# Stacking B with K and U with V on the partitions of a chunked recurrence, and moving part of the state work among the grams

## Chip, cores and metric

One core of a Trainium2 chip. The metric is the device time of one execution in microseconds, lower is better. All arithmetic of the part in question is fp32.

## What is computed

The program is three layers on 1024 latent and 256 context tokens of width 1024. The change touches only the recurrence of the first layer, an RWKV-7 scan over 1280 tokens with 8 heads of 64, run in both directions:

```python
def step(S, inp):
    r_t, w_t, k_t, v_t, a_t, b_t = inp
    sa = jnp.einsum('bhij,bhj->bhi', S, a_t)
    S = S * w_t[:, :, None, :] + sa[..., None] * b_t[:, :, None, :] + v_t[..., None] * k_t[:, :, None, :]
    return S, jnp.einsum('bhij,bhj->bhi', S, r_t)
```

## The kernel before, in words

The recurrence is `phase_scan` (line 822). It runs alone: a barrier of all engines ends the phase before and the one after begins behind another. The tokens are cut in chunks of 64; two chunks make a block of 128 tokens, and there are 10 blocks. Both directions (d = 0 forward, 1 backward) go side by side on the same engines. Inside a block, chunk q lies on partitions 64q to 64q+63. An fp32 matmul shows in the trace as two weight loads and two matmuls, on separate rows (PEld and PE).

For each block there is "new" work, which needs no state, and for the block before it "old" work, which carries the state. They are interleaved by hand: each engine has a loop over n from 0 to 10 whose body is a fixed list of calls, new ones for block n and old ones for block n-1. Engines wait for one another by semaphores (`done(engine, name, d, n, r)`); within an engine the order is the list's.

New work of block n:

- SP loads A and R (`ar`, line 880), B and K (`bk`, 884) and V (`vt`, 886), transposed, that is channels on partitions, three DMAs for each direction; a block's loads are issued one block ahead. Before the first gram come also six constants (line 896), which stand on SP's queue after the loads of block 0.
- `gram(n, 0)` multiplies B, `gram(n, 1)` K, with A and R together (line 929), in 64x64 tiles: 64 matmuls in all. VectorE's `masked` (1131) multiplies each PSUM bank by a triangular mask, giving `mB` and `mK`. K's gram waits for B's masks, since both use the banks bA and bB.
- `turn_v` and `turn_bk` transpose V (937), B and K (947) to tokens on partitions; ScalarE copies them out (`turned_v`, `turned_bk`, recorded at 1246, like all its copies). `mask_v` (958) multiplies K's masked gram by V; ScalarE copies the product to `MV`.
- The inverse of the unit triangular matrix of each chunk is built up: ScalarE copies the 32x32 diagonal blocks (`diagonal`), VectorE makes the start value (`base`), GpSimd (1120) the block products' left operand. Then four levels: `level_p` (972), VectorE's mask (1150), `level_z` (982), VectorE's sum and transpose (1158, 1160), each with a copy of half of Z by ScalarE (`swapped`). At the end `last_p` (994) and `last_z` (1006) in 32x32 tiles.

Old work, twice a block (e = 0, 1, one chunk each), each time four steps of TensorE that depend on one another: `state_w` (1024), VectorE adds MV (1184); `state_u` (1037), ScalarE copies U; `state_sums` (1055), 64 matmuls in 64x64 tiles that add U and V parts in PSUM; `state_read` (1063). VectorE then renews the state (1189, 1194) and adds the output (1200). The lists of before put W of e = 0 behind `level_p(n, 0)`, and the others one by one behind the groups that follow.

The gram of block n+1 waits for `zf` of block n, VectorE's last step (1173).

## Time and profile before

| | us |
|---|---|
| median of 3 runs (3467.09 to 3473.81) | 3473.52 |
| the profiled execution's own time | 3474.22 |
| its span | 3472.4 |
| the recurrence in it, first load issued to last output | 595.3 to 1090.7 |

The profile is of one execution. Times in it count from the span's start. PE is TensorE's matmuls, PEld its weight loads, DVE VectorE, ACT ScalarE, SP the queue that issues DMAs. In the timeline a row is one instruction or a run of like ones (x count), and a bracket says how long the engine was idle before it and what ended that; "issue" means that nothing which the profile shows held it. In the windows view a row is a stretch with the busy time of each engine and, in brackets, its instructions, the granted TensorE clock (1.00 is 2.4 GHz), the share of DMA engines busy and GB/s.

### The profile page before, as it was taken

The page shows a single profiled execution, that of the slowest core. Times are in us where ns is not written, and L with a number is a line of the kernel's source. Part 1 is how long each engine was busy: PE and PEld are TensorE (multiplying, and loading weights), DVE is VectorE, ACT ScalarE, POOL GpSimd, SP SyncE. Part 2 cuts the span into 40 slices and gives each one's busy share as a digit, 9 for nine tenths or more (in the row PEclk, how much of TensorE's full clock was granted, in tenths as well). Part 3 has the DMA queues.
Part 4 walks back from the last instruction along what each step waited for, and adds up shares of the span by engine and source line. Part 5 has one row for each costly group of instructions (what it writes and reads, how often), then busy time and mean ns, then how long its engine had stood idle before and what let it go on. Part 6 is the DMA issues. An engine that isn't in the chain of part 4 may idle for free. (4 is left out here: it accounts for less than half of the span.)

```text
span 3472.4 us, 63359 instructions
## 1 busy us (share of the span) xinstructions
PE 3105.7 (89%) x27018; PEld 2569.8 (74%) x27018; DVE 2013.4 (58%) x2899; ACT 1442.3 (42%) x2207; POOL 409.7 (12%) x293
## 2 busy tenths in 40 slices
PE   8999997777775799898999999999677899999999
PEld 5878886766664679766899987777445778888887
DVE  6746345566564532253555534666343588888787
ACT  4434433333332333256444432443354454545443
POOL 0122221000000122110000012312011100000000
PEclk9999999798897899999999999999898999999999
DMA  8432223233214221324211114112111322222853
GB/s 295 137 127 105 97 90 131 63 76 76 76 46 155 103 86 42 140 75 162 81 60 54 42 37 146 58 52 97 59 49 34 125 79 79 85 79 73 303 164 122
DMA packets 184566, 343.88 MB, mean 99 GB/s; under 512 B 11488, under 2 KB 116064, under 8 KB 180832
## 3 DMA queue, kind: packets, MB, share of 16 engines
q1 hardware_dynamic: 161248, 252.80, 21.8%
q0 software_dynamic: 23040, 87.04, 7.4%
q8 instruction: 215, 3.52, 0.4%
q14 instruction: 63, 0.52, 0.1%
HBM read 243.72 MB, written 96.08 MB: 98 GB/s over the span
## 5 line engine op out<-in xcount | busy, mean ns | idle before, releaser
L60 PE MATMUL ev_ps<-h_hi,even_ring_hi 128*128 128x512 f32 (+1 forms) x792 | 288.0, 364 | 1.3 <-DVE late_area L806 1.3
L61 PE MATMUL ev_ps<-h_lo,even_ring_hi 128*128 128x512 f32 (+1 forms) x792 | 280.4, 354 | 0.0
L62 PE MATMUL ev_ps<-h_hi,even_ring_lo 128*128 128x512 f32 (+1 forms) x792 | 280.4, 354 | 0.0
L60 PE MATMUL ff_ps<-ff_op,ff_w_hi 128*128 128x512 f32 x672 | 263.5, 392 | 13.6 <-DVE ff_w_lo L3504 10.7
L62 PE MATMUL ff_ps<-ff_op,ff_w_lo 128*128 128x512 f32 x672 | 262.8, 391 | 0.0
L61 PE MATMUL ff_ps<-ff_op,ff_w_hi 128*128 128x512 f32 x672 | 262.7, 391 | 0.0
L60 PEld LDWEIGHTS ev_ps<-h_hi,even_ring_hi 128*128 128x128 f32 x792 | 149.6, 189 | 39.9 <-issue 19.6
L3071 ACT ACTIVATE ma_e<-ma_s,ma_nm 128x1280 f32<-128x1280 f32 x64 | 84.9, 1327 | 216.3 <-DVE ma_nm L3107 216.3
L61 PEld LDWEIGHTS ev_ps<-h_lo,even_ring_hi 128*128 128x128 f32 x792 | 149.7, 189 | 21.7 <-issue 1.7
L62 PEld LDWEIGHTS ev_ps<-h_hi,even_ring_lo 128*128 128x128 f32 x792 | 149.6, 189 | 21.3
L60 PEld LDWEIGHTS ff_ps<-ff_op,ff_w_hi 128*128 128x128 f32 x672 | 127.1, 189 | 41.2 <-DVE ff_w_lo L3504 14.5
L3045 PE MATMUL ma_o<-ma_pt,ma_v 128*128 128x128 f32 x1280 | 153.2, 275 | 0.0
L3045 PEld LDWEIGHTS ma_o<-ma_pt,ma_v 128*128 128x128 f32 x1280 | 147.9, 192 | 0.0
L61 PEld LDWEIGHTS ff_ps<-ff_op,ff_w_hi 128*128 128x128 f32 x672 | 127.0, 189 | 26.6 <-issue 0.2
L62 PEld LDWEIGHTS ff_ps<-ff_op,ff_w_lo 128*128 128x128 f32 x672 | 126.9, 189 | 26.5
L103 POOL TENSOR_TENSOR even_ring_lo<-even_ring_raw,even_ring_hi 128x1024 fp32r<-128x1024 f32 x33 | 94.2, 2854 | 417.3 <-ACT even_ring_hi L98 417.3
L60 PE MATMUL ff_ps<-ff_w_hi 128*128 128x512 f32 x336 | 131.2, 390 | 2.6 <-DVE ff_w_lo L3584 1.8
L62 PE MATMUL ff_ps<-ff_w_hi,ff_w_lo 128*128 128x512 f32 x336 | 130.8, 389 | 0.0
L61 PE MATMUL ff_ps<-ff_w_lo,ff_w_hi 128*128 128x512 f32 x336 | 130.7, 389 | 0.0
L3537 DVE SCALAR_TENSOR_TENSOR h<-h,cols 128x1023 f32<-128x1023 f32 x96 | 122.6, 1278 | 0.5 <-ACT h L3401 0.4
L3103 DVE TENSOR_REDUCE ma_mx<-ma_s 128x1 f32<-128x1024 f32 x64 | 78.2, 1222 | 69.7 <-PE ma_s L3025 69.7
L103 POOL TENSOR_TENSOR second_ring_lo<-second_ring_raw,second_ring_hi 128x1024 fp32r<-128x1024 f32 x32 | 79.1, 2473 | 307.9 <-ACT second_ring_hi L98 307.9
(566 smaller groups left out, 8362.3 us busy)
## 6 DMA issues: line engine op xcount, KB each, us to landing
w_up_raw<-in_w_up SPq DMA_DIRECT2D x48, 512.0 KB, 4.6
w_up_raw<-in_w_down SPq DMA_DIRECT2D x34, 512.0 KB, 5.0
even_ring_raw<-in_ev_w_in POOLq DMA_DIRECT2D x33, 512.0 KB, 3.9
late_area<-in_ada_w SPq DMA_DIRECT2D x32, 512.0 KB, 5.2
ffn_mid<-h POOLq DMA_DIRECT2D x24, 512.0 KB, 2.9
ff_mem<-ffn_mid SPq DMA_DIRECT2D x24, 512.0 KB, 11.0
ar<-late_area SPq DMA_DIRECT2D x8, 1280.0 KB, 5.6
bk<-late_area SPq DMA_DIRECT2D x8, 1280.0 KB, 8.0
```

The lines of the kernel that those rows point to most:

```text
L60: nc.tensor.matmul(out, w_hi, x_hi, start=start, stop=False, skip_group_check=resumed)
L61: nc.tensor.matmul(out, w_hi, x_lo, start=False, stop=False, skip_group_check=resumed)
L62: return nc.tensor.matmul(out, w_lo, x_hi, start=False, stop=stop, skip_group_check=resumed)
L103: nc.gpsimd.tensor_tensor(ring.lo[:, a % 2], ring.w[:], ring.hi[:, a % 2].bitcast(F32), ALU.subtract).then_inc(ring.lo_done, 1)
L3045: mm = nc.tensor.matmul(po[:, u % 2, 0:P], v[:, h % 2, t], pt[:, u % 2, t * P:t * P + P], start=t == 0, stop=t == NT - 1)
L3071: nc.scalar.activation(e[:, s % 2], ps[:, 0:T], ACT.Exp, bias=nm[:, s % 2:s % 2 + 1], accum_out=sm[:, s % 2:s % 2 + 1]).then_inc(exps, 1)
L3103: nc.vector.tensor_reduce(mx[:, b, 0:1], ps[:, 0:2 * BANK], AX, ALU.max).then_inc(maxed, 1)
L3537: stt(out=a[:, i:LAT], in0=rows[x_][:, 0:LAT - i], scalar=col(g, "conv_ffn_w", 48 * (2 - i) + at), in1=a[:, i:LAT], op0=ALU.mult, op1=ALU. ...
```

## The change

B and K of a chunk are stacked: `bk` holds, for each pair of heads and chunk q, 64 tokens of one beside 64 of the other (K first for q = 1), so one matmul of 64x128 tiles gives both grams of a chunk. `gram(n, x)` over B and K becomes `gram(n, q)` over the chunks, 32 matmuls instead of 64. The two masked grams lie stacked in `M`, on 128 partitions, and U and V of a chunk in `UV`: U on the half of the chunk, V on the other. `state_sums` then contracts over 128 partitions, one matmul where two were added in PSUM: 32 matmuls for each e instead of 64, in 128x64 tiles. V's loads swap the chunks of a block. The loads of `bk` and `vt` are cut by chunk: seven DMAs for each direction and block instead of three, with rows of 64 tokens instead of 128. ScalarE copies V in four pieces of 64 partitions, and the diagonal blocks of chunk 0 before those of chunk 1; GpSimd's product is made for each chunk.

The lists change too. On TensorE `state_w(n-1, 0)` goes between the two grams, `state_u(n-1, 0)` between `turn_v` and `turn_bk`, `state_sums(n-1, 0)` ahead of `level_p(n, 0)` and `state_read(n-1, 0)` behind it; the second half's W and U follow levels 1 and 2, its sums `level_p(n, 3)`. VectorE and ScalarE follow.

```diff
-        ar, bk, vt = sb("ar", [P, 3, 2, 4, 2, P]), sb("bk", [P, 2, 2, 4, 2, P]), sb("vt", [P, 2, 2, 4, P])
-        mB, mK = sb("mB", [P, 2, 2, 8, 2, CH]), sb("mK", [P, 2, 2, 8, 2, CH])
-        V, Bt, MV, Zf = sb("V", [P, 2, 2, BANK]), sb("Bt", [P, 2, 2, 2, BANK]), sb("MV", [P, 2, 2, BANK]), sb("Zf", [P, 2, 2, 8, CH])
+        ar, bk, vt = sb("ar", [P, 3, 2, 4, 2, P]), sb("bk", [P, 2, 2, 4, 2, 2, CH]), sb("vt", [P, 2, 2, 4, P])
+        M, UV = sb("M", [P, 2, 2, 2, 8, 2, CH]), sb("UV", [P, 2, 2, 2, 8, CH])
+        Bt, MV, Zf = sb("Bt", [P, 2, 2, 2, BANK]), sb("MV", [P, 2, 2, BANK]), sb("Zf", [P, 2, 2, 8, CH])
         dg, Z, X, P5 = (sb(x, [P, 2, 8, 32]) for x in ("diag", "Z", "X", "P5"))
         mD, Pm = sb("mD", [P, 2, 8, CH]), sb("Pm", [P, 2, 8, CH])
         Zs = sb("Z_swapped", [P, 2, 4, 32])
-        W, U = sb("W", [P, 2, BANK]), sb("U", [P, 2, BANK])
+        W = sb("W", [P, 2, BANK])
...
-                        sp.dma_start(bk[:, n % 2, d].rearrange("c p k t -> c (p k) t"),
-                                     g.bkT[d].rearrange("c p k t -> c (p k) t")[:, :, at:at + P]).then_inc(ld[d, n % 2], 16)
-                        sp.dma_start(vt[:, n % 2, d], g.vT[:, :, at:at + P]).then_inc(ld[d, n % 2], 16)
+                        for q in range(2):
+                            to = at + CH * q
+                            for x in range(2):
+                                sp.dma_start(bk[:, n % 2, d, :, q, x ^ q], g.bkT[d][:, :, x, to:to + CH]).then_inc(ld[d, n % 2], 16)
+                            sp.dma_start(vt[:, n % 2, d, :, half(1 - q)], g.vT[:, :, to:to + CH]).then_inc(ld[d, n % 2], 16)
...
-                def gram(n, x):
+                def gram(n, q):
                     for d in range(2):
-                        if x == 0:
-                            pe.wait_ge(ld[d, n % 2], 48 * (n // 2 + 1))
+                        if q == 0:
+                            pe.wait_ge(ld[d, n % 2], 112 * (n // 2 + 1))
                             if n:
                                 done(pe, "Pev", d, n - 1)
                                 done(pe, "zf", d, n - 1)
                         else:
-                            done(pe, "mB", d, n)
+                            done(pe, "mk0", d, n)
                         settle()
                         for p in range(4):
-                            for q in range(2):
-                                for h in range(2):
-                                    r, c = half(h), half(q)
-                                    last = mm((bA, bB)[h][d][c, 128 * p:128 * p + 128], bk[r, n % 2, d, p, x, c], ar[r, n % 3, d, p, :, c],
-                                              start=True, stop=True)
-                        last.then_inc(S[("gB", "gK")[x], d], 2)
+                            for h in range(2):
+                                r, c = half(h), half(q)
+                                last = mm((bA, bB)[h][d][:, 128 * p:128 * p + 128], bk[r, n % 2, d, p, q].rearrange("c x t -> c (x t)"),
+                                          ar[r, n % 3, d, p, :, c], start=True, stop=True)
+                        last.then_inc(S[("g0", "g1")[q], d], 2)
...
-                            last = nc.tensor.transpose((bB, bA)[x][d][:, 128 * p:128 * p + 128], bk[:, n % 2, d, p, x], g.ident[:])
+                            last = nc.tensor.transpose((bB, bA)[x][d][:, 128 * p:128 * p + 128],
+                                                       bk[:, n % 2, d, p, x].rearrange("c x t -> c (x t)"), g.ident[:])
...
-                        for j, (p, h) in enumerate(HEADS):
+                        for j in range(8):
                             for q in range(2):
-                                c = half(q)
-                                last = mm(bB[d][c, 64 * j:64 * j + 64], mK[c, n % 2, d, j, 0],
-                                          V[c, n % 2, d, 128 * p + 64 * h:128 * p + 64 * h + 64], start=True, stop=True)
+                                k = half(1 - q)
+                                last = mm(bB[d][half(q), 64 * j:64 * j + 64], M[k, n % 2, d, q, j, 0], UV[k, n % 2, d, q, j],
+                                          start=True, stop=True)
...
-                        for x in (2, 3, 0, 1):
-                            for h in range(2):
-                                for d in range(2):
-                                    c, r, j = half(ORDER[d][e]), half(h), 4 * h + p
-                                    o, ov = half(j), half(2 * p + h)
-                                    at = 64 * p + (256 if x >= 2 else 0)
-                                    lhs, rhs = ((U[c, d, o], mB[c, b, d, j, 1]), (V[c, b, d, ov], mK[c, b, d, j, 1]),
-                                                (Bt[c, b, d, 0, ov], U[c, d, o]), (Bt[c, b, d, 1, ov], V[c, b, d, ov]))[x]
-                                    mm(bD[d][r, at:at + 64], lhs, rhs, start=x % 2 == 0, stop=x % 2 == 1)
+                        for h in range(2):
+                            for d in range(2):
+                                q, r, j = ORDER[d][e], half(h), 4 * h + p
+                                mm(bD[d][r, 256 + 64 * p:320 + 64 * p], Bt[:, b, d, q, half(2 * p + h)], UV[:, b, d, q, j], start=True, stop=True)
+                        for h in range(2):
+                            for d in range(2):
+                                q, r, j = ORDER[d][e], half(h), 4 * h + p
+                                mm(bD[d][r, 64 * p:64 * p + 64], UV[:, b, d, q, j], M[:, b, d, q, j, 1], start=True, stop=True)
...
                     if new:
                         gram(n, 0)
+                    if old:
+                        state_w(n - 1, 0)
+                    if new:
                         gram(n, 1)
                         turn_v(n)
+                    if old:
+                        state_u(n - 1, 0)
+                    if new:
                         turn_bk(n, 0)
                         mask_v(n)
                         turn_bk(n, 1)
-                        level_p(n, 0)
-                    if old:
-                        state_w(n - 1, 0)
-                    if new:
-                        level_z(n, 0)
-                    if old:
-                        state_u(n - 1, 0)
-                    if new:
-                        level_p(n, 1)
                     if old:
                         state_sums(n - 1, 0)
                     if new:
+                        level_p(n, 0)
+                    if old:
+                        state_read(n - 1, 0)
+                    if new:
+                        level_z(n, 0)
+                        level_p(n, 1)
                         level_z(n, 1)
                     if old:
-                        state_read(n - 1, 0)
+                        state_w(n - 1, 1)
                     if new:
                         level_p(n, 2)
                         level_z(n, 2)
                     if old:
-                        state_w(n - 1, 1)
+                        state_u(n - 1, 1)
                     if new:
                         level_p(n, 3)
                     if old:
-                        state_u(n - 1, 1)
+                        state_sums(n - 1, 1)
                     if new:
                         level_z(n, 3)
-                    if old:
-                        state_sums(n - 1, 1)
-                    if new:
                         last_p(n)
...
-                        done(pool, "mB", d, n)
                         if n:
                             done(pool, "P", d, n - 1, NL - 1)
-                        nc.gpsimd.tensor_tensor(mD[:, d], mB[:, n % 2, d, :, 0], hm[:].unsqueeze(1).broadcast_to([P, 8, CH]),
-                                                ALU.mult).then_inc(S["blocks", d], 1)
+                        for q in range(2):
+                            c = half(q)
+                            done(pool, ("mk0", "mk1")[q], d, n)
+                            nc.gpsimd.tensor_tensor(mD[c, d], M[c, n % 2, d, q, :, 0], hm[c].unsqueeze(1).broadcast_to([CH, 8, CH]),
+                                                    ALU.mult).then_inc(S["blocks", d], 1)
...
                         masked(n, 0, 0)
                         masked(n, 0, 1)
+                    if old:
+                        state_w(n - 1, 0)
+                    if new:
                         masked(n, 1, 0)
                         masked(n, 1, 1)
                         base(n)
                         level_mask(n, 0)
                     if old:
-                        state_w(n - 1, 0)
+                        state_s(n - 1, 0)
                     if new:
                         level_add(n, 0)
+                    if old:
+                        output(n - 1, 0)
+                    if new:
                         level_mask(n, 1)
                         level_add(n, 1)
                     if old:
-                        state_s(n - 1, 0)
+                        state_w(n - 1, 1)
                     if new:
                         level_mask(n, 2)
-                    if old:
-                        output(n - 1, 0)
-                    if new:
                         level_add(n, 2)
-                    if old:
-                        state_w(n - 1, 1)
-                    if new:
                         level_mask(n, 3)
                         level_add(n, 3)
                         inverse_diagonal(n)
...
-                    for d in range(2):
-                        done(act, "mB", d, n)
-                        if n:
-                            done(act, "z0", d, n - 1)
-                        for c in range(4):
-                            k, a = slice(32 * c, 32 * c + 32), 32 * (c % 2)
-                            cp(dg[k, d], mB[k, n % 2, d, :, 0, a:a + 32]).then_inc(S["diag", d], 1)
+                    for q in range(2):
+                        for d in range(2):
+                            done(act, ("mk0", "mk1")[q], d, n)
+                            if n and q == 0:
+                                done(act, "z0", d, n - 1)
+                            for c in (2 * q, 2 * q + 1):
+                                k, a = slice(32 * c, 32 * c + 32), 32 * (c % 2)
+                                cp(dg[k, d], M[k, n % 2, d, q, :, 0, a:a + 32]).then_inc(S["diag", d], 1)
 
                 def turned_v(n):
                     for d in range(2):
                         done(act, "trV", d, n)
-                        cp(V[:, n % 2, d], bA[d][:]).then_inc(S["Vev", d], 1)
+                        for q in range(2):
+                            k = half(1 - q)
+                            cp(UV[k, n % 2, d, q].rearrange("s (h p) c -> s h p c", h=2),
+                               bA[d][k].rearrange("s (p h c) -> s h p c", p=4, h=2)).then_inc(S["Vev", d], 1)
...
-                        cp(U[c, d], bC[d][c]).then_inc(S["Uev", d], 1)
+                        cp(UV[c, n % 2, d, ORDER[d][e]].rearrange("s j c -> s (j c)"), bC[d][c]).then_inc(S["Uev", d], 1)
...
                         diagonal(n)
                         turned_v(n)
+                    if old:
+                        state_u(n - 1, 0)
+                    if new:
                         turned_bk(n, 0)
                         masked_v(n)
                         turned_bk(n, 1)
                         swapped(n, 0)
                     if old:
-                        state_u(n - 1, 0)
+                        output(n - 1, 0)
                     if new:
                         swapped(n, 1)
                         swapped(n, 2)
                     if old:
-                        output(n - 1, 0)
+                        state_u(n - 1, 1)
                     if new:
                         swapped(n, 3)
-                    if old:
-                        state_u(n - 1, 1)
-                    if new:
                         corner(n)
```

## Rows read from the trace of the kernel before

**Rows 1.** The page's first part, busy us, share of the span, instructions, by engine

```profile
PE 3105.7 (89%) x27018; PEld 2569.8 (74%) x27018; DVE 2013.4 (58%) x2899; ACT 1442.3 (42%) x2207; POOL 409.7 (12%) x293
```

**Rows 2.** Windows: stretch, us, busy of PE, PEld, DVE, ACT, POOL, clock, DMA, GB/s

```profile
645.60:1063.70 418.10, 315.45 (x11736) 288.48 (x11736) 251.43 (x559) 153.54 (x378) 22.56 (x18) 0.88 0.23 58
...
786.26:798.68 12.42, 9.73 (x216) 8.12 (x217) 7.98 (x17) 7.25 (x16) 2.51 (x2) 1.00 0.97 244
...
798.69:831.98 33.29, 24.57 (x1088) 23.12 (x1089) 19.87 (x46) 9.77 (x27) 0.00 (x0) 0.84 0.04 9
...
1063.70:1090.70 27.00, 15.86 (x448) 14.82 (x448) 7.21 (x20) 3.68 (x8) 0.00 (x0) 0.62 0.08 22
```

**Rows 3.** Timeline of weight loads: start, us, what; in brackets idle before

```profile
757.11 0.13 PEld L982 LDWEIGHTS sc_bAB<-sc_Z_swapped,sc_Pm 64*64 64x64 f32 x1 [1.75 <-issue]
...
760.81 0.14 PEld L1055 LDWEIGHTS sc_bD<-sc_U,sc_Bt 64*64 64x64 f32 x2 [0.67 <-issue]
...
708.02 0.30 PEld L972 LDWEIGHTS sc_bAB<-sc_X,sc_mD 64*64 64x64 f32 x10 [2.18 <-issue]
```

**Rows 4.** Windows of weight loads, from one stall's end to the next stall's

```profile
757.11:760.80 3.69, 2.52 (x125) 1.00 0.02 4
...
760.81:764.16 3.35, 1.96 (x128) 1.00 0.02 5
...
779.97:783.82 3.85, 2.66 (x127) 1.00 0.02 4
```

**Rows 5.** Windows: line 1055 alone, and one level of block 0 with all engines

```profile
760.80:762.90 2.10, 2.08 (x124) 1.94 (x124) 1.00 0.03 8
...
622.50:625.90 3.40, 2.42 (x128) 2.26 (x128) 2.24 (x5) 2.19 (x7) 0.00 (x0) 1.00 0.76 211
```

**Rows 6.** Timeline of TensorE in the front, and at the end of that block

```profile
786.26 1.98 PE L929 MATMUL sc_bAB<-sc_ar,sc_bk 64*64 64x128 f32 x64 [0.96 <-DVE sc_Zf L1173]
...
794.81 1.35 PE L958 MATMUL sc_bAB<-sc_V,sc_mK 64*64 64x64 f32 x38 [0.44 <-issue]
...
829.85 1.74 PE L1006 MATMUL sc_bAB<-sc_Z,sc_P 32*32 32x32 f32 x64
```

**Rows 7.** Timeline of VectorE in the front: both groups of masks

```profile
788.30 1.89 DVE L1131 TENSOR_TENSOR sc_mB<-sc_bAB,sc_m 128x512 f32<-128x512 f32 x3 [0.18 <-PE sc_bAB L929]
...
791.77 1.89 DVE L1131 TENSOR_TENSOR sc_mK<-sc_bAB,sc_m 128x512 f32<-128x512 f32 x3 [0.18 <-PE sc_bAB L929]
```

**Rows 8.** Timeline of ScalarE in the front, then U's copies (lines by form)

```profile
789.62 3.49 ACT L1246 ACTIVATE sc_diag<-sc_mB 32x256 f32<-32x256 f32 x8 [4.78 <-DVE sc_mB L1131]
...
793.13 1.08 ACT L1246 ACTIVATE sc_V<-sc_bAB 128x512 f32<-128x512 f32 x2
...
L1246 ACT ACTIVATE sc_U<-sc_bC 64x512 f32<-64x512 f32 x28 | 16.6, 591 | 53.7 <-PE sc_bC L1037 53.3
```

**Rows 9.** The state's W: TensorE in a window of line 1024, one VectorE add

```profile
753.90:754.80 0.90, 0.69 (x32) 0.59 (x32) 1.00 0.13 29
...
801.74 0.42 DVE L1184 TENSOR_TENSOR sc_W<-sc_bC,sc_MV 64x256 f32<-64x256 f32 x1 [1.03 <-PE sc_bD L1024]
```

**Rows 10.** DMA issues of bk and vt; the window of one block's loads

```profile
sc_bk<-bk SPq DMA_DIRECT2D x20, 512.0 KB, 6.3
...
sc_vt<-v_even SPq DMA_DIRECT2D x20, 256.0 KB, 7.3
...
742.90:752.90 10.00, 7.65 (x156) 6.27 (x152) 6.49 (x13) 7.16 (x16) 2.51 (x2) 1.00 1.11 275
```

**Rows 11.** The start: SP's issue of the last constant, TensorE's first gram

```profile
604.95 0.43 SPq L896 DMA_DIRECT2D sc_eye<-in_eye  x1
...
608.90 2.41 PE L929 MATMUL sc_bAB<-sc_ar,sc_bk 64*64 64x128 f32 x40 [18.44 <-DMA sc_eye<-in_eye]
```

**Rows 12.** Windows at the lower clock: after the stall, and two levels of block 0

```profile
708.77:712.10 3.33, 3.19 (x107) 3.08 (x98) 3.09 (x9) 0.00 (x0) 0.00 (x0) 0.50 0.02 5
...
632.70:641.40 8.70, 8.19 (x256) 7.75 (x256) 6.07 (x13) 1.93 (x7) 0.00 (x0) 0.50 0.02 4
```

More of the change, by code:

```diff
@@ L827, in phase_scan @@
     NBC = CTX // P
-    names = ["gB", "gK", "trV", "trBK", "MV", "P", "Z", "lastP", "lastZ", "W", "U", "YS",
-             "mB", "mK", "z0", "Zbase", "X", "Pm", "Zadd", "zdiag", "zf", "Wev", "stmp", "snew", "y",
+    names = ["g0", "g1", "trV", "trBK", "MV", "P", "Z", "lastP", "lastZ", "W", "U", "YS",
+             "mk0", "mk1", "z0", "Zbase", "X", "Pm", "Zadd", "zdiag", "zf", "Wev", "stmp", "snew", "y",
              "diag", "blocks", "Uev", "Vev", "BKev", "MVev", "Pev", "y1", "Zs"]
-    reps = {"Zs": 2 * NL, "gB": 2, "gK": 2, "mB": 2, "mK": 2, "trBK": 2, "BKev": 2, "P": NL, "Z": NL, "Pm": NL, "Zadd": NL, "X": NL + 1, "diag": 4,
+    reps = {"Zs": 2 * NL, "g0": 2, "g1": 2, "mk0": 2, "mk1": 2, "Vev": 2, "blocks": 2, "trBK": 2, "BKev": 2, "P": NL, "Z": NL, "Pm": NL, "Zadd": NL, "X": NL + 1, "diag": 4,
             "W": 2, "U": 2, "YS": 2, "Wev": 4, "Uev": 2, "stmp": 2, "snew": 2, "y1": 2, "y": 2}
@@ L942, in turn_bk @@
                         if x == 0:
-                            done(pe, "mK", d, n, 1)
+                            done(pe, "mk1", d, n, 1)
                         else:
```

12 lines of the change are left out of this document (6 added, 6 removed).

## Prediction, before the changed kernel was run

> **What bounds it now.** The page's engine table [rows 1] puts TensorE at 89% of the span, but that mean says nothing about the recurrence, the only phase touched. The windows view cuts it out [rows 2]. Between 645.60 and 1063.70 us nine blocks, each carrying new work and the state work of the block before, take 418.1 us, 46.5 us a block, and TensorE is at work for 315 of them; VectorE for 251, ScalarE for 154. No engine is full, so I look for what TensorE waits for, stage by stage. A block has two stages. In the front (12.4 us, grams to the second pair of transposes) it issues 217 weight loads. In the rest (33.3 us, first `level_p` to `last_z`, the dense part) it issues 1088.
>
> The weight-load timeline of the dense part shows idle stretches of 0.7 to 2.2 us ended by "issue", by nobody's semaphore [rows 3]. They fall in the middle of a run of like instructions. The windows laid from one stall's end to the next [rows 4] count 125 to 128 weight loads each time, with as many matmuls, and last 3.35 to 3.85 us at the full clock. The work does not need that long: the 128 loads and matmuls of a level keep TensorE at work for 2.42 us [rows 5]. So a fixed number of instructions, about 256, comes at best every 3.4 to 3.9 us. I read this as TensorE waiting for its program. It fits the whole dense part: 1088/128 = 8.5 portions in 33.3 us, 3.9 each. The Trainium skill ("Runtime: NRT & Kernel Launch", Instruction fetch mechanics) says fetch comes in blocks of 256 instructions but is mostly hidden, with room for 2048 in TensorE's buffer. The size agrees with the trace, the hiding does not; by the rule the idle time would have another cause, and that is a rival below.
>
> In the front TensorE waits for VectorE's masks, then for ScalarE's copies [rows 6 to 8].
>
> **The change, part by part.** Per block, counted in weight loads (two for each fp32 matmul):
>
> *Grams stacked.* 128 loads become 64. Now 64 of 64x64 tiles with 128 columns take 1.98 us with four tiles working at once [rows 6]. The new form covers two of the four tiles with one instruction, so half as many at twice the share: I take 1.98 us again. The bounds are 0.99 us (an instruction costs what it cost) and 2.4 us. Gain 0: array time is not saved, only instructions.
>
> *State sums stacked.* 128 loads become 64, twice a block. Now 124 take 2.08 us at the full clock [rows 5], 17 ns each. In 128x64 tiles two work at once instead of four, so I take 30 ns each, 1.9 us, again no gain; bounds 1.0 and 2.6 us. Three changes of tile form a block are added in the dense part; the one from 64x64 to 32x32 at 829.85 loses the overlap that neighbours have [rows 6], about 0.1 us. Together 0.3 us.
>
> *Front, worked through from the first gram (0 = 786.26).* The first four masks end at 790.19, +3.9 [rows 7]. Direction-wise W of the old block now comes here: 0.7 us of TensorE [rows 9] in its 1.5 us wait, costing nothing; on VectorE four adds, 0.42 each, 1.5 us [rows 9], so to 5.4. The other gram is done by then. Four masks more, 0.69 + 3 x 0.60 = 2.5, end at 7.9 instead of 7.4: +0.5. ScalarE is worse off. Its eight `diag` copies used to start on the first masks and take 3.49 us [rows 8], ending at 6.9; now four of them need the second masks, start at 7.3 and end at 9.0. V becomes four copies on 64 partitions instead of two on 128. A 64x512 copy takes 591 ns [rows 8], as long as one on 128, so 2.4 us instead of 1.08: 11.4. Ahead of B's copy now stand U's two, 1.2 us [rows 8]: 12.6, B's first to 13.2. `mask_v` waits for V and B: 13.3 instead of 8.55 (794.81). So the front is longer by 4.8 us, nearly all on ScalarE. TensorE fills part of it with U0 (32 loads like W0, 0.7 us) and idles some 3.7 us after the first transposes. From `mask_v` to `level_p` it was 3.9 us (794.81 to 798.69), 0.5 us of that for ScalarE; with the first sums between, 1.9 us, it becomes some 5.2. `level_p` then starts at 18.5 at the latest instead of 12.4; since the sums also cover the wait for B's last copies, 18.0. Front: +5.6 us.
>
> *Dense part.* W0 (32), U0 (32) and sums0 (128) have left it and sums1 loses 64: 1088 - 256 = 832 loads, 6.5 portions. At 3.9 us each that is 25.4 us; plus 0.3 for the tile forms and 0.5 for the read and W between levels, 26.2 instead of 33.3: -7.1 us. The lower bound is the chain of dependences: one level without state work takes 3.4 us [rows 5], four of them 13.6, and last products, reads, W1, U1 and sums1 some 9: 22.5 us, also 6.5 x 3.45. The upper bound leaves the stalls and takes off only what W0, U0 and sums0 held, 0.7 + 0.7 + 2.1 and the 1.5 us of W on VectorE, in part side by side: 4.5 us, 28.8.
>
> *Masks' consumers.* GpSimd's two block products become four on half the partitions, 2.5 to 5.0 us [rows 10], from 7.3 to some 12 in the block, wanted at 18: nothing; cover gone, they would cost 2.5. `W1`, `U1` and the outputs move a level, none late.
>
> *DMAs.* Per block and direction, three loads become seven. They are issued a block ahead and took 10 us of a 46 us block [rows 10]; at rows of 256 B the 1.5 MB of bk and vt (of 2.5) could at worst take twice as long, 16 us: still hidden. The start has no cover. The constants stand behind load(0) on SP's queue, and the first gram waited 18.4 us for the last of them [rows 11]. Eight more issues at the shortest seen, 0.43 us [rows 11], are 3.4 us; partly these lie beside the transfers. Bounds: 0, and 60% of the 9 us of transfer, +5.4. I take +3. The Trainium skill ("DMA: Bandwidth & Descriptors", Specifications) asks for 512 B or more for line rate; by it the start would cost the +5.4.
>
> *First and last pass.* Block 0 has no state work: front +3.3 (second `diag` half and V), levels not held up by portions. +3. The last pass (27 us for 448 loads at a clock of 0.62 [rows 2]) is a chain; its sums are as long: 0.
>
> **Sum.** Nine blocks at +5.6 - 7.1 = -1.5: -13.5. Start +3, block 0 +3: -7.5; I round to -8 and set it against the profiled execution, 3474.2 us (span 3472.4), 0.7 above the median of 3473.5. That gives 3466.
>
> **Rivals.**
> *Clock falls in the new gap.* TensorE's granted clock is 1.0 or 0.5 of 2.4 GHz by stretch. It fell right after the 2.2 us stall that ended at 708.02 [rows 3, 12], and was 0.50 through block 0's levels, where no state work lies between them [rows 12]. The change makes both: an idle stretch of 3.7 us, and levels 0 and 1 with less between them. At 0.5 the level's pair of groups takes 4.35 us instead of 3.4 [rows 12, 5], hardly more than the 3.9 a portion takes anyway, so a fall there costs little; a fall at 13 us of the block, before `mask_v`, transposes and sums0, costs some 2 to 3 us of their 5. Nine times 2.3: +21, 3487. It decides from an idle stretch of about 2 us on. Against it: the front that I read kept a clock of 1.00 with a gap of 1.5 us in it [rows 2].
> *The stalls are not the program's.* By the skill's rule fewer instructions gain nothing: dense part 28.8, so +1.1 a block, +10, start and block 0 +6: 3490. Against it stands the count of 125 to 128 in all five intervals that I laid out (three stand in rows 4).
> *A smaller effect of both signs.* A third of the clock's cost, 8 us: 3474, no difference (chance: all but 0.02 of it within 0.2%).
> *Faster.* If portions come every 3.45 us once the half-clock stretches are fewer, or a stacked sum costs what an unstacked instruction did, 2.5 to 3.5 us a block more: 3440.
> *The change doesn't halve the time of what it halves* is already in the sum.
>
> **Chances.** Forecast 0.38, clock 0.25, not the program's 0.07, between 0.15, faster 0.15. A measurement of this kernel tells 0.2%, 7 us, from nothing. The forecast lies at that edge and gives 0.27 to faster and 0.11 to same; with the others: faster 0.43, same 0.24, slower 0.33. The range, from 3440 to 3492, takes in the faster case and the slower ones; 3455 to 3475 is the forecast's own.
>
> **What would show it.** Intervals of 128 loads at 3.4 to 3.9 us still, but fewer: 8.7 portions a block. L1055's successor with 64 loads in about 1.9 us. `mask_v` 13 us after the first gram, ScalarE without a pause from the second `diag` to B's copy. Block period 45.0 us. First gram 3 us later after the first load's issue. Wrong if the period grows, with a granted clock under 0.85, or if `mask_v` starts by 10 us.

## The result, and the profile after

| | before | after |
|---|---|---|
| median us (4 runs each) | 3473.47 (3467.09 to 3473.81) | 3501.67 (3500.55 to 3502.52) |
| the profiled execution's own time / span | 3474.22 / 3472.4 | 3501.81 / 3499.7 |

The changed kernel is slower: ratio 1.0083, 95% interval 1.0069 to 1.0097. The forecast was 3466, and 3501.67 lies above its range too.

The page of the changed kernel, its engines and its queue of instructions (packets, MB, share), answers to [rows 1]:

```profile
PE 3136.1 (90%) x25098; PEld 2606.0 (74%) x25098; DVE 2036.3 (58%) x2899; ACT 1455.3 (42%) x2227; POOL 436.2 (12%) x313
...
q8 instruction: 201, 3.29, 0.4%
```

TensorE has 1920 matmul records fewer and yet is busy 30 us longer. The first sign that the program fetch was read rightly stands in the second row: the page of before has 215 packets and 3.52 MB there, 14 packets of 16 KB more.

Windows of the changed kernel, columns as in [rows 2]: its blocks 1 to 9, then block 4's front and dense part, then the last pass.

```profile
650.81:1092.78 441.97, 347.42 (x10009) 323.07 (x10009) 271.99 (x559) 165.53 (x396) 46.80 (x36) 0.79 0.24 54
801.46:823.49 22.03, 16.73 (x280) 15.34 (x280) 11.90 (x21) 11.46 (x24) 5.20 (x4) 0.78 0.65 144
823.50:850.11 26.61, 21.19 (x835) 20.11 (x833) 18.45 (x42) 6.96 (x20) 0.00 (x0) 0.81 0.02 5
1092.78:1118.30 25.52, 17.06 (x320) 15.94 (x320) 5.12 (x14) 3.02 (x6) 0.00 (x0) 0.57 0.08 22
```

Nine blocks take 442.0 us where they took 418.1 [rows 2], on 1727 fewer matmul records, and the granted clock is 0.79 where it was 0.88. The dense part is shorter as expected (26.6 instead of 33.3 us). The front is 22.0 us instead of 12.4, and its clock of 0.78 is far from the 1.00 of [rows 2].

TensorE's timeline shows where in the front:

```profile
801.46 3.31 PE L930 MATMUL sc_bAB<-sc_ar,sc_bk 64*128 64x128 f32 x32 [0.23 <-DVE sc_Zf L1176]
...
806.25 2.06 PE L930 MATMUL sc_bAB<-sc_ar,sc_bk 64*128 64x128 f32 x32 [0.85 <-DVE sc_M L1134]
...
816.10 3.68 PE L960 MATMUL sc_bAB<-sc_UV,sc_M 64*64 64x64 f32 x64 [3.82 <-ACT sc_Bt L1249]
...
819.71 1.79 PE L948 MATMUL sc_bAB<-ident_sb,sc_bk 128*128 128x128 f32 x8
```

and the windows of three of its stretches, columns as above:

```profile
806.20:808.40 2.20, 2.06 (x32) 1.89 (x32) 2.14 (x6) 1.60 (x4) 1.27 (x1) 1.00 1.19 288
...
791.40:793.40 2.00, 2.00 (x64) 1.97 (x64) 0.71 (x2) 1.16 (x4) 0.00 (x0) 1.00 0.03 8
...
816.00:819.80 3.80, 3.70 (x65) 3.61 (x66) 0.00 (x0) 1.09 (x3) 0.00 (x0) 0.50 0.22 48
```

The gap of 3.82 us ahead of `mask_v` is the one that the prediction foresaw (3.7). What runs behind it runs at 1.2 GHz (granted 0.50): `mask_v` takes 3.68 us, the transposes 1.79. In each of blocks 1 to 9 `mask_v` ran at a mean granted clock of 0.50 to 0.57. At 2.4 GHz the same code takes 2.08 and 1.10 us in another run (experiment e4_warm, below). The second gram, at 2.4 GHz, takes 2.06 us with half of the instructions, and the 64 of stacked sums 2.10 from first start to last end (the window in the second row closes 0.1 us before that): those two estimates held.

ScalarE in that front:

```profile
806.13 1.74 ACT L1249 ACTIVATE sc_diag<-sc_M 32x256 f32<-32x256 f32 x4 [6.09 <-DVE sc_M L1134]
810.10 1.73 ACT L1249 ACTIVATE sc_diag<-sc_M 32x256 f32<-32x256 f32 x4 [2.23 <-DVE sc_M L1134]
811.85 2.44 ACT L1249 ACTIVATE sc_UV<-sc_bAB 64x512 f32<-64x512 f32 x4
814.19 1.20 ACT L1249 ACTIVATE sc_UV<-sc_bC 64x512 f32<-64x512 f32 x2
815.41 1.08 ACT L1249 ACTIVATE sc_Bt<-sc_bAB 128x512 f32<-128x512 f32 x2
```

It runs without a pause from 810.10 to 816.5, and `mask_v` waits at its end. V's four copies stand behind the second half of `diag`, though V's transposes were there from 810.2 on. From here on, "front" is from the first gram to `level_p(n, 0)` and "dense" is from there to the next block's first gram, each a mean over blocks 1 to 8 of the profiled execution.

| us | before | after | difference | forecast |
|---|---|---|---|---|
| issue of the first load to first gram | 13.6 | 15.4 | +1.8 | +3 |
| block 0 | 36.7 | 42.8 | +6.1 | +3 |
| blocks 1 to 9 | 418.1 | 442.0 | +23.9 | -13.5 |
| last pass, to TensorE's last matmul | 24.9 | 25.5 | +0.6 | 0 |

Together +32.4. The recurrence began 2.7 us earlier in this trace and the phases behind it are 2.4 us shorter, though the change leaves both parts alone: 27.3 us of span.

### The profile page after: what moved, and what is told of

It is laid out like the page before. It is cut to its first block and busy times, and to the rows that moved or that the text cites. A ratio compares the mean times of both kernels' runs of the same rounds, so it can differ in the third digit from the quotient of the medians.

```text
span 3499.7 us, 59639 instructions
## 1 busy us (share of the span) xinstructions
PE 3136.1 (90%) x25098; PEld 2606.0 (74%) x25098; DVE 2036.3 (58%) x2899; ACT 1455.3 (42%) x2227; POOL 436.2 (12%) x313
## 5 line engine op out<-in xcount | busy, mean ns | idle before, releaser
L60 PE MATMUL ff_ps<-ff_op,ff_w_hi 128*128 128x512 f32 x672 | 263.4, 392 | 13.6 <-DVE ff_w_lo L3511 10.7
L61 PEld LDWEIGHTS ff_ps<-ff_op,ff_w_hi 128*128 128x128 f32 x672 | 127.0, 189 | 26.6 <-issue 0.2
L62 PEld LDWEIGHTS ff_ps<-ff_op,ff_w_lo 128*128 128x128 f32 x672 | 126.8, 189 | 26.6
## 6 DMA issues: line engine op xcount, KB each, us to landing
ff_mem<-ffn_mid SPq DMA_DIRECT2D x24, 512.0 KB, 10.9
```

The lines of the kernel that those rows point to most:

```text
L60: nc.tensor.matmul(out, w_hi, x_hi, start=start, stop=False, skip_group_check=resumed)
L61: nc.tensor.matmul(out, w_hi, x_lo, start=False, stop=False, skip_group_check=resumed)
L62: return nc.tensor.matmul(out, w_lo, x_hi, start=False, stop=stop, skip_group_check=resumed)
```

## The experiments

Two theories of these 32 us of the recurrence. *Clock*: the gap that ScalarE makes ahead of `mask_v` drops TensorE to 1.2 GHz, and the work behind it, up to the next gram, pays. *Order*: the moved state work itself (sums and U in the front, thinner levels) costs it, whatever the clock. The runs below were measured beside the kernel before on the same chip, whose medians were 3474.78 (e1 to e4), 3470.72 (e6 to e9) and 3466.16 (e10 to e13). First all of them, with the stages of the profile. The stages come from one profiled execution of each, the medians from 4 to 10 executions that spread by 2 to 21 us, so differences of a few tenths of a us a block say nothing by themselves.

| run | median us | ratio, 95% | block | `mask_v` after gram | front | dense | clock front / dense |
|---|---|---|---|---|---|---|---|
| before | | | 46.5 | 9.7 | 13.1 | 33.4 | 0.91 / 0.87 |
| after | 3501.67 | 1.0083 (1.0069 to 1.0097) | 48.9 | 14.4 | 21.8 | 27.1 | 0.80 / 0.79 |
| e1_lists_only | 3479.48 | 1.0012 (1.0003 to 1.0021) | 47.4 | 11.8 | 17.0 | 30.5 | 0.90 / 0.74 |
| e2_stack_only | 3476.75 | 1.0008 (0.9999 to 1.0018) | 46.1 | 11.9 | 16.9 | 29.2 | 0.85 / 0.90 |
| e3_act_order | 3453.34 | 0.9936 (0.9920 to 0.9953) | 43.6 | 10.9 | 16.5 | 27.1 | 0.93 / 0.77 |
| e4_warm | 3469.69 | 0.9986 (0.9973 to 1.0000) | 45.6 | 13.8 | 19.3 | 26.3 | 0.96 / 0.79 |
| e6_sums_in_levels | 3461.55 | 0.9973 (0.9959 to 0.9987) | 44.8 | 11.1 | 16.1 | 28.7 | 0.91 / 0.79 |
| e7_by_direction | 3463.46 | 0.9978 (0.9966 to 0.9990) | 44.5 | 10.9 | 17.6 | 26.9 | 0.93 / 0.80 |
| e8_fill_gap | 3463.02 | 0.9973 (0.9962 to 0.9984) | 44.9 | 11.4 | 18.1 | 26.8 | 0.89 / 0.76 |
| e9_stack_act | 3447.63 | 0.9933 (0.9919 to 0.9948) | 42.7 | 9.5 | 13.3 | 29.4 | 0.98 / 0.89 |
| e10_before_act | 3491.97 | 1.0077 (1.0062 to 1.0092) | 47.7 | 9.8 | 15.5 | 32.2 | 0.88 / 0.86 |
| e11_diag_dve | 3445.98 | 0.9941 (0.9925 to 0.9958) | 43.5 | 9.5 | 13.6 | 30.0 | 0.98 / 0.86 |
| e12_many_small | 3456.93 | 0.9975 (0.9966 to 0.9985) | 44.9 | 9.5 | 13.3 | 31.6 | 0.98 / 0.90 |
| e13_few_wide | 3451.29 | 0.9961 (0.9948 to 0.9974) | 43.6 | 9.5 | 13.3 | 30.3 | 0.98 / 0.91 |

**The two halves of the change apart.** e1_lists_only is the kernel before with the changed lists of TensorE, VectorE and ScalarE and nothing stacked; e2_stack_only is the changed kernel with the lists of before.

```diff
 # e1, TensorE's list of before.py (e2: the same lines the other way round, in after.py)
                     if new:
                         gram(n, 0)
+                    if old:
+                        state_w(n - 1, 0)
+                    if new:
                         gram(n, 1)
                         turn_v(n)
...
```

> The kernel before with the changed kernel's three lists, nothing stacked. Theory (ScalarE's longer queue in the front plus a clock fall in the gap cost more than the saved portions of 256 instructions give): here V is still two copies and all eight diagonal copies start on the first masks, so mask_v starts about 10 us after the first gram instead of 14.6, the clock stays at 1.00 in the front, and the dense part loses 192 of 1088 weight loads (1.5 portions): block about 44 us, 3450 us in all, faster than both. Rival A (the moved state work is what hurts, because it stood in useful places before and kept the clock up between the levels): 3485 or more. Rival B (the lists do nothing): 3473.

> The changed kernel's stacking with the lists of before. Theory: ScalarE still makes four copies of V and the late diagonal copies, so mask_v starts 11.5 to 12 us after the first gram (8.55 before), with a gap of some 3 us that lets the clock fall; the dense part has 960 weight loads (7.5 portions of 3.9 us, 29 us): block 46 to 47.5 us, 3475 to 3490 us. Rival A (the lists do the harm): 3465 or less. Rival C (the stacked matmuls are slow by their form): above 3500, with the sums' 64 matmuls well over 2.1 us at the full clock.

Each half alone makes the recurrence no faster (+0.12% and +0.08%), and together they cost 0.83%. So there is something between them. e2 came out as expected. e1 was expected at 3450 and missed by 29 us: `mask_v` came at +11.8 instead of +10, and the dense part, 1.5 portions lighter, gained only 2.9 us, at a granted clock of 0.74. Its 3479 lies between rival B (3473) and rival A (3485 or more), so with the moved lists part of what the lighter dense part should give is lost. Windows of eight blocks in each, columns as before:

```profile
641.10:1020.60 379.50, 302.59 (x10435) 281.42 (x10435) 222.81 (x495) 137.76 (x336) 20.04 (x16) 0.80 0.24 62
```

```profile
649.40:1017.80 368.40, 282.22 (x8896) 259.01 (x8896) 241.55 (x495) 146.93 (x352) 41.57 (x32) 0.88 0.28 63
```

The first row is of e1, the second of e2. The lists alone bring the clock of a whole block to 0.80, the stacking alone leaves it at 0.88, as it was [rows 2]. The table says which stage: every run with the moved lists (e6 has them in part) has 0.74 to 0.80 in the dense part, every run with the lists of before 0.86 to 0.91.

**ScalarE's order.** In e3_act_order only ScalarE's list of the changed kernel is another: V and B are copied before the second half of `diag`, and U after it.

```diff
-                        diagonal(n)
-                        turned_v(n)
-                    if old:
-                        state_u(n - 1, 0)
-                    if new:
-                        turned_bk(n, 0)
+                        diagonal(n, 0)
+                        turned_v(n)
+                        turned_bk(n, 0)
+                        diagonal(n, 1)
+                    if old:
+                        state_u(n - 1, 0)
+                    if new:
                         masked_v(n)
```

> The changed kernel with ScalarE's list alone reordered: V's and B's (first) copies ahead of the second chunk's diagonal copies and of U's copies. Theory: 1.7 + 1.2 us leave the way to mask_v, which starts at 10 to 11 us instead of 14.6; the idle gap of TensorE shrinks below 1.5 us and the clock stays up in the front; block 44 to 45.5 us, 3455 to 3470 us. Rival C (slow forms) or rival A (lists): no more than the 3 us of order per block come back at best and the clock stays as it is, 3490 to 3500.

This turns the loss into a gain, 3501.67 to 3453.34 us, 2 us below what was expected. ScalarE's timeline of e3, and the windows of the same block's front and dense part:

```profile
919.45 2.44 ACT L1249 ACTIVATE sc_UV<-sc_bAB 64x512 f32<-64x512 f32 x4 [1.75 <-PE sc_bAB L938]
921.79 1.06 ACT L1249 ACTIVATE sc_Bt<-sc_bAB 128x512 f32<-128x512 f32 x2
922.88 1.72 ACT L1249 ACTIVATE sc_diag<-sc_M 32x256 f32<-32x256 f32 x4
```

```profile
912.54:927.95 15.41, 13.21 (x280) 11.84 (x280) 9.73 (x21) 9.90 (x21) 5.07 (x4) 1.00 0.91 201
927.96:955.50 27.54, 22.99 (x835) 21.67 (x832) 18.45 (x42) 8.18 (x24) 0.00 (x0) 0.74 0.03 7
```

V's copies now wait for TensorE's transposes and for nothing else. `mask_v` starts 9.9 us after this gram, and the gap ahead of it is 0.36 us instead of 3.82. The moved work stands where it stood, and its dense part has the low clock still (0.77); so the *Order* theory doesn't account for the loss.

**The same gap, filled.** e4_warm leaves ScalarE's order as in the changed kernel and only gives TensorE something to do while it waits: eight matmuls whose results nobody reads.

```diff
+                def keep_busy(n):
+                    for j in range(8):
+                        d = j % 2
+                        nc.tensor.matmul(bC[d][half(1 - ORDER[d][0]), 0:256], g.ident[half(0), 0:CH],
+                                         m1[half(0)].rearrange("s d k t -> s (d k t)"), start=True, stop=True)
...
                         turn_bk(n, 0)
+                        keep_busy(n)
                         mask_v(n)
```

> The changed kernel with eight filler matmuls (64x64 tile, 256 columns, fp32, into a free half of the state's bank) put on TensorE between turn_bk(n, 0) and mask_v, where it idles 3.8 us. They add 16 weight loads a block. Theory with the clock as the second half of the loss: mask_v, transposes and sums0 run at the full clock, mask_v's 64 matmuls in 2.1 us instead of 3.7, ScalarE's queue is as before; 2 to 3 us a block come back, 3475 to 3483 us. Rival (the clock costs nothing, since it is ScalarE that is waited for): 3500 or slower.

TensorE does more and the kernel is 32 us faster than the changed one, 3469.69, more than the 19 to 27 us that were expected. No wait was shortened by hand, since ScalarE's queue is the same, row for row, only with its times:

```profile
891.48 2.44 ACT L1256 ACTIVATE sc_UV<-sc_bAB 64x512 f32<-64x512 f32 x4
...
895.04 1.09 ACT L1256 ACTIVATE sc_Bt<-sc_bAB 128x512 f32<-128x512 f32 x2
```

```profile
882.34:900.82 18.48, 15.05 (x296) 12.88 (x295) 11.36 (x20) 11.31 (x24) 5.21 (x4) 1.00 0.72 173
900.83:926.98 26.15, 21.03 (x837) 20.12 (x834) 18.56 (x42) 6.99 (x21) 0.00 (x0) 0.80 0.02 4
```

```profile
891.84 1.94 PE L955 MATMUL sc_bC<-sc_m,ident_sb 64*64 64x256 f32 x16
895.73 2.08 PE L966 MATMUL sc_bAB<-sc_UV,sc_M 64*64 64x64 f32 x64 [1.95 <-issue]
897.75 1.10 PE L948 MATMUL sc_bAB<-ident_sb,sc_bk 128*128 128x128 f32 x8
```

These are the fillers, `mask_v` and the transposes behind it, on TensorE. The fillers split the gap: 1.95 us of it are left.

With the clock at 1.00 through the front, this block has `mask_v` at +13.39 and `level_p` at +18.49; the prediction had 13.3 and 18.0. Five of the blocks 1 to 8 look like this one, with a period of 44.6 us where 45.0 was forecast. So the clock is worth 48.9 - 45.6 = 3.3 us a block. Without most of its fall the kernel is 5 us faster than before, where 8 were forecast; the interval, 0.9973 to 1.0000, just touches no difference.

**Attempts to have both.** Three runs on e3 tried to bring the dense part's clock back, or the rest of the gap down. e6 puts the first sums behind `level_p(n, 0)` again, and their read behind `level_z(n, 0)`; e7 copies on ScalarE V and B of direction 0, then of direction 1; e8 is e7 with two of e4's fillers.

```diff
 # e6, TensorE
-                        state_sums(n - 1, 0)
                         level_p(n, 0)
+                        state_sums(n - 1, 0)
-                        state_read(n - 1, 0)
                         level_z(n, 0)
+                        state_read(n - 1, 0)
 # e7, ScalarE
-                        turned_v(n)
-                        turned_bk(n, 0)
+                        for d in range(2):
+                            turned_v(n, d)
+                            turned_bk(n, 0, d)
```

> e3_act_order with the first sums and read moved back between the levels (sums behind level_p(n, 0), read behind level_z(n, 0); VectorE's and ScalarE's lists follow). Theory (portions of 256 instructions at 3.9 us set the dense part, whatever stands in it): level_p starts 2 us sooner, 13.5 us, the dense part has 896 instead of 832 weight loads, half a portion more, 2 us: as e3_act_order, 3446 to 3460 us. Rival A (state work between the levels fills waits for VectorE and keeps the clock up): dense part no longer than 27.5 us, mean clock there over 0.85, 3440 or less.

> e3_act_order with ScalarE's copies of V and B taken direction by direction (V0, B0, V1, B1). If ScalarE's queue still sets the start of mask_v, it starts 0.6 to 1.2 us sooner, 8.9 to 9.3 us after the first gram in blocks whose front is at the full clock, and the whole is 0 to 10 us faster than e3_act_order, 3443 to 3453. If TensorE's transposes set it by now, no difference.

> e7_by_direction with two filler matmuls (256 columns) ahead of mask_v. The remaining gap is under 1.5 us. If the clock still falls in some fronts because of it (as in half of the blocks of e3_act_order), the fillers bring 0 to 5 us; if those falls come from the levels before, nothing, or 0 to 5 us slower by the fillers' own 0.4 us a block.

All three are faster than before, and by their intervals all three are slower than e3 (whose four runs were on another chip). So e6 and e7 missed what was expected of them, 3446 to 3460 and 3443 to 3453, and e8's fillers bring nothing over e7. Sums between two levels (e6) leave the dense clock at 0.79. By direction (e7), ScalarE idles 1.1 us behind V0, waiting for B's transposes, and `level_p` comes 1 us later. The runs of e6 scatter over 21 us (3450.40 to 3471.40); in its profile the clock falls in five of nine fronts. Whether the scatter comes from that is open, and nothing finer can be read from these three.

**The better combination.** e9_stack_act joins the two halves that had shown themselves good: stacked operands, the lists of before, and V and B ahead of the second half of `diag` on ScalarE.

```diff
 # e2, ScalarE
-                        diagonal(n)
+                        diagonal(n, 0)
                         turned_v(n)
                         turned_bk(n, 0)
+                        diagonal(n, 1)
                         masked_v(n)
```

> e2_stack_only (stacked, lists of before) with ScalarE's copies of V and B ahead of the second chunk's diagonal copies. Theory: mask_v starts 9.5 to 10 us after the first gram instead of 11.7, the gap shrinks and the clock stays at 1.00 there; dense part as in e2, 29 us (960 weight loads): block 43.5 to 44.5 us, 3450 to 3460 us, so the stacking alone is a gain once ScalarE's order fits it. Rival (the moved lists are needed for the gain): 3470 or more.

It has the lowest ratio of the study, at 3447.63 us 0.67% below before, 2 us better than expected. e3, with the moved lists, stands at 0.9936 (0.64% below), inside its interval: once ScalarE's order is right, the moved lists neither gain nor cost anything that these runs can tell. The blocks of 42.7 and 43.6 us in the table don't decide between them, since e9's profile is of the fastest of its four executions (3442.93) and e3's of the slowest (3457.41). Windows of e9's blocks 1 to 8, and of one block's front and dense part:

```profile
646.00:987.50 341.50, 270.77 (x8898) 248.80 (x8897) 226.32 (x495) 144.71 (x352) 40.52 (x32) 0.91 0.31 68
902.66:915.71 13.05, 9.66 (x155) 8.28 (x153) 8.57 (x17) 8.31 (x18) 5.07 (x4) 1.00 0.98 209
915.72:945.40 29.68, 24.40 (x960) 22.90 (x960) 20.00 (x47) 9.77 (x27) 0.00 (x0) 0.88 0.10 19
```

From block 2 on every front is the same to 0.01 us, with `mask_v` at +9.23 and `level_p` at +13.06, at a clock of 1.00: 13.1 us, as long as the mean of before. The dense part issues 960 loads instead of 1088 and takes 29.4 us instead of 33.4.

Two controls. e10_before_act puts V and B ahead of all eight `diag` copies in the kernel before, with nothing stacked; e11_diag_dve takes the second half of `diag` off e9's ScalarE and gives it to VectorE.

```diff
 # e10, before.py, ScalarE
-                        diagonal(n)
                         turned_v(n)
                         turned_bk(n, 0)
+                        diagonal(n)
 # e11, in VectorE's base()
+                        done(dve, "mk1", d, n)
+                        for c in (2, 3):
+                            k, a = slice(32 * c, 32 * c + 32), 32 * (c % 2)
+                            nc.vector.tensor_copy(dg[k, d], M[k, n % 2, d, 1, :, 0, a:a + 32]).then_inc(S["diag", d], 1)
```

> Control: the kernel before with ScalarE's copies of V and B put ahead of all diagonal copies, nothing stacked, lists of TensorE and VectorE unchanged. If the gain of e9_stack_act came from ScalarE's order alone, this is at 3450 too. Theory (the gain is the stacking's fewer instructions, which ScalarE's order had hidden): the dense part keeps its 1088 weight loads and 33 us; mask_v starts up to 0.9 us sooner, but the start values come 1 us later, as all eight diagonal copies stand behind; 3468 to 3482 us, no gain.

> e9_stack_act with the second chunk's diagonal copies moved from ScalarE (1.7 us) to VectorE, which stood idle for 3 us there. Theory: the copies of MV and B's second pair come up to 0.8 us sooner, and level_p no longer waits for the start values: it begins 0.5 to 0.8 us sooner in each block, 3438 to 3445 us. If the dense part's portions swallow that, as e9_stack_act.

e10 is 0.77% slower than before: `mask_v` is where it was (+9.8, before +9.7), and the start values of the levels, behind all eight `diag` copies, are late (`level_p` +15.5 instead of +13.1). It was expected at 3468 to 3482 and came out at 3491.97. So this order is no gain of its own; in the stacked kernel it mends what the stacking does to ScalarE's queue. The control isn't e9's order exactly, which keeps half of `diag` ahead of V; that split in the kernel before was not run. e11 gains nothing over e9 (0.9941 against 0.9933, intervals overlapping), where 3 to 10 us were expected: with these copies on VectorE, `level_p` comes at +13.36 instead of +13.06.

**Instructions against array time.** In e9 TensorE gets work that nobody reads, between the first sums and `level_z(n, 1)`: 32 matmuls of 16 columns (64 loads) in e12, 8 of 256 columns (16 loads) in e13. The diff is e12's.

```diff
+                def filler(n):
+                    for j in range(32):
+                        d = j % 2
+                        o = half(ORDER[d][0])
+                        nc.tensor.matmul(bC[d][o, 256:256 + 16], g.ident[o, 0:CH],
+                                         m1[o].rearrange("s d k t -> s (d k t)")[:, 0:16], start=True, stop=True)
...
+                        if old:
+                            filler(n)
                         level_z(n, 1)
```

> e9_stack_act with 32 filler matmuls of 16 columns (64 weight loads, 64 matmuls in the trace) between sums0 and level_z(n, 1) in the dense part. Portion theory: 128 instructions more are half a portion, 1.9 us a block, 17 us in all over e9_stack_act, more than e13_few_wide costs, though its columns are a quarter. Rival (the stalls have nothing to do with the number of instructions): the fillers' own time on the array, about 1 us a block at 15 ns each, 9 us, and no more stalls than e9_stack_act.

> e9_stack_act with 8 filler matmuls of 256 columns (16 weight loads, 16 matmuls) in the same place: about 1.7 to 2 us of array time a block in two tiles, but only 32 instructions, an eighth of a portion (0.5 us). Portion theory: the array time lies in what would have been a stall, so it costs 0.5 to 1 us a block, 5 to 9 us over e9_stack_act, less than e12_many_small. Rival (array time is what counts in the dense part): 16 us over e9_stack_act, and more than e12_many_small.

Windows of blocks 1 to 8 in e12 and in e13, against 341.50 us in e9:

```profile
647.90:1006.60 358.70, 286.02 (x9411) 263.61 (x9410) 225.50 (x495) 144.75 (x352) 40.48 (x32) 0.92 0.30 65
...
647.60:996.10 348.50, 279.22 (x9026) 253.81 (x9026) 225.27 (x495) 144.75 (x352) 40.49 (x32) 0.93 0.30 67
```

The dense part grows by 2.15 us in e12 (29.41 to 31.56) and by 0.86 in e13 (to 30.27). If each instruction costs its share of a portion of 3.92 us, 64 loads are 1.96 and 16 are 0.49 us. By array time the two should be nearly alike: the fillers hold TensorE for 2.2 us in e12 and 2.0 in e13, from first start to last end in one block of each. The difference between them is 1.29 us; 48 loads are worth 1.47 us by portions, array time 0.2. So in these profiles it is the instructions that the dense part pays for, and e13's wide matmuls found room in the stalls for over half of their time. e12 taken alone would not show it, since its array time is as long as its share of a portion. The medians bear out the sign and not the size. e12 is 5.6 us slower than e13 on the same chip, 0.6 us a block where the profiles have 1.29, and their ratios' intervals overlap; over e9 they are 15 and 10 us slower by the ratios, where 17 and 5 to 9 were expected.

## Why the prediction was wrong, step by step

**Failed: the clock's fall in the new gap.** The prediction named this mechanism among its rivals, "Nine times 2.3: +21, 3487", gave it 0.25, and worked the forecast's front at the full clock with the note that the front it had read "kept a clock of 1.00 with a gap of 1.5 us in it". The gap of 3.7 us that it had itself worked out (3.82 measured) was over its own point of decision, "an idle stretch of about 2 us", and there was one trace row of a fall behind a shorter stall [rows 3, 12]. The likeliest case was thus set against its own evidence. Its price was too low as well: 3.3 us a block by e4, 32 us in all by the medians, against 2.3 and 21. Of e4's 3.3 us, 1.9 lie between `mask_v` and `level_p`, 0.6 ahead of `mask_v` and 0.8 in the dense part; only the first had been priced, and for `mask_v` and the transposes behind it 2.3 was right (3.68 + 1.79 us against 2.08 + 1.10). The front grew by 8.6 us, not 5.6. `mask_v` came at +14.4, not 13.3, because in five of eight blocks the first gram still ran at the low clock that the block before had left (3.21 to 3.78 us instead of 2.06); where it did not, `mask_v` was at +13.39 to 13.41. From `mask_v` to `level_p` it took 7.3 us, not 4.7, with `mask_v` and the transposes at 1.2 GHz. The base was read too well, too: the front of 12.4 us at a clock of 1.00 [rows 2] is one of four such among the ten of before, and the mean over blocks 1 to 8 was 13.1 us at 0.91. Block 0, with a gap of 3.49 us and no dense state work, paid 6.1 us, not 3.

**Underrated: that a thinner dense part lowers the clock again.** The rival said of a fall in the levels that it "costs little", since a portion takes 3.9 us anyway. That is nearly so, since 6.5 portions at 4.17 us are 27.1 us where 26.2 was forecast. In differences it is -6.3 for -7.1. But the low clock of a thin stretch reaches over into the next block's gram, and that had no term. What exactly in the levels makes it fall was not settled: e6, with sums between two levels, did not lift it.

**Right.** ScalarE as the engine that sets `mask_v`, with every copy in the order and length worked out (V in four of 0.6 us, U's two, then B). The array rates: halving the instructions of the grams (2.06 us for 1.98) and sums (2.1 for 1.9) saves no array time. The dense part by portions: 832/128 of them. In the changed kernel two stalls stand 126 loads apart, in the middle of like instructions; between them lie shorter idle times of 0.2 to 0.65 us, and the portion takes 4.90 us:

```profile
827.28 0.13 PEld L984 LDWEIGHTS sc_bAB<-sc_Z,sc_Pm 64*64 64x64 f32 x1 [0.97 <-issue]
...
832.19 0.18 PEld L984 LDWEIGHTS sc_bAB<-sc_Z_swapped,sc_Pm 64*64 64x64 f32 x1 [1.12 <-issue]
```

```profile
827.28:832.18 4.90, 2.79 (x126) 2.43 (x126) 4.00 (x10) 1.84 (x6) 0.00 (x0) 0.92 0.02 5
```

The trace also keeps when each 16 KB packet of the instruction queue (q8 on the page) started and how long it took, and that shows what the prediction could only infer. Around these two stalls packets start at 824.91 and 829.81 us, also 4.90 us apart; they land at 825.86 and 830.68, and the stalls end 1.4 and 1.5 us later. In the dense parts of blocks 1 to 8 of before, packets start 3.44 to 4.98 us apart, 3.85 in the mean, and 31 of the 37 idle times of the weight loads over 1 us end 1.2 to 1.6 us after a packet has landed. In after it is 7 of 18, at 4.24 us in the mean: there more of the idle time has other causes. Before used 82 packets for blocks 1 to 8, after and e9 71, e13 72 and e12 75, one for every 125 to 127 weight loads with as many matmuls.

e9 gives the cleanest reading: 960 loads, 7.5 portions, 29.4 us, 3.92 each, where before had 8.5 at 3.93. The Trainium skill ("Runtime: NRT & Kernel Launch", Instruction fetch mechanics) calls such fetch mostly hidden; these stretches show it in the open. The start cost +1.8 us, inside its bounds of 0 and 5.4.

**Not the cause.** The rival that the stalls are not the program's had a dense part of 28.8 us; it measured 27.1 in after, at a lower clock than it assumed. The products on GpSimd stayed hidden, as forecast, though at the longer of the two figures (5.2 us, forecast 2.5 to 5.0).

## What to carry to other kernels

When a change opens an idle gap on TensorE, work out the length of the gap and then the sum a second time with everything behind it at 1.2 GHz; a gap of 3.8 us here cost 3.3 us a block more than its own length. Look in the queue of the engine that the gap waits for before accepting it: here six small copies in a better order were worth 48 us (the changed kernel to e3) and 26 us (e2 to e9, by their ratios), about what the change lost, or more. When work is moved between stages, look at the granted clock of the stage that it leaves: here it fell from 0.86 to 0.91 down to 0.74 to 0.80 in the dense part, though e3 and e9 show no net loss by it once the gap was gone.

## What the runs showed beyond that

Work that nobody reads can make a kernel faster: e4's eight matmuls a block took 32 us off, but removing the gap (e3) took off 48.

VectorE slowed down beside GpSimd. Its two additions of `eye`, 128x256, took 0.76 us in before and 0.75 in e3, where no product ran beside them; in the changed kernel they ran for the most part beside GpSimd's products (810.15 to 814.2) and took 1.81:

```profile
813.03 1.81 DVE L1145 TENSOR_TENSOR sc_Z<-sc_Z,sc_eye 128x256 f32<-128x256 f32 x2
```

```profile
810.15 4.08 POOL L1123 TENSOR_TENSOR sc_mD<-sc_M,sc_hm 64x512 f32<-64x512 f32 x3 [2.63 <-DVE sc_M L1134]
```

It lay beside ScalarE's longer queue and cost nothing here. A product on 64 partitions takes GpSimd 1.3 us, as long as one on 128 [rows 10], and the same is true of ScalarE's copies: halving the partitions halves nothing.
